# Two-block network on one core: output units of the merge as 512 + 256 columns, an earlier table load with six stores, and half-row transposes in the linear attention

## The reference

```
mixed = (sigmoid(g_a) * (y_a @ w_a) + sigmoid(g_b) * (y_b @ w_b))      # 256 x 2048
y = mixed @ w_out
x = rmsnorm(x + gate * y, final_g)
```

## Time and profile before

| | |
|---|---|
| runs | 2350.02 us median of 3 (2348.01 to 2352.76) |
| profiled execution | 2346.09 us, its span 2344.2 us |
| TensorE busy | 2285.3 us (97%), 23364 matmuls |
| VectorE, ScalarE, GpSimd busy | 1223.2, 1178.7, 1342.1 us |
| granted TensorE clock | 0.995 of full speed in the mean |
| DMA | 360.70 MB, 154 GB/s in the mean |

### The profile page before, as it was taken

One profiled execution on the slowest core, in us unless ns is written; L12 is line 12 of the kernel. 1 busy time (PEld: TensorE's weight loads), 2 busy tenths in 40 slices (PEclk: granted clock), 3 DMA queues, 4 the chain that ended last, 5 costly groups with the idle time before them and its releaser, 6 DMA issues.

```text
span 2344.2 us, 60261 instructions
## 1 busy us (share of the span) xinstructions
PE 2285.3 (97%) x23364; PEld 1944.4 (83%) x23364; DVE 1223.2 (52%) x2449; ACT 1178.7 (50%) x1999; POOL 1342.1 (57%) x566
## 2 busy tenths in 40 slices
PE   6999999999999999999999999999999999999997
PEld 4787787778777888899999888888888888888886
DVE  2478778877883323466565455453444533333322
ACT  3244545454554444444444555555555555555554
POOL 1112123212332344478888878777777877778785
PEclk8999999999999999999999999999999999999999
DMA  9922112211211223267776555555555555555553
GB/s 389 381 87 66 40 60 77 66 41 58 70 65 50 81 99 108 99 222 251 256 252 244 183 166 176 168 173 173 177 172 171 181 169 172 177 177 172 170 181 134
DMA packets 101244, 360.70 MB, mean 154 GB/s; under 512 B 11184, under 2 KB 14768, under 8 KB 101072
## 3 DMA queue, kind: packets, MB, share of 16 engines
q1 hardware_dynamic: 99872, 356.89, 44.4%
q10 hardware_dynamic: 1200, 1.25, 0.2%
HBM read 356.00 MB, written 2.10 MB: 153 GB/s over the span
## 4 chain that ended last, share of the span: by engine, by line
PE 89%; DVE 2%; ACT 2%; issue 1%; DVEq 0%; ACTq 0%
PE ps L223 32%; PE ps L224 16%; PE ps L684 5%; PE ps L196 4%; PE ps L198 4%; PE ps L197 4%; PE ps L686 4%; PE ps L685 4%; PE ps L815 1%; PE ps L800 1%; PE ps L836 1%; PE ps L980 1%; PE ps L850 1%; PE ps L951 1%; PE ps L1000 1%
## 5 line engine op out<-in xcount | busy, mean ns | idle before, releaser
L187 POOL TENSOR_TENSOR wlo<-raw,whi 128x1024 fp32r<-128x1024 f32 x555 | 1336.7, 2422 | 948.7 <-ACT whi L178 898.7
L223 PE MATMUL ps<-acts,whi 128*128 128x512 f32 x3072 | 1087.6, 398 | 1.3 <-DVE acts L2794 1.3
L224 PE MATMUL ps<-acts,wlo 128*128 128x256 f32 x3072 | 856.7, 279 | 0.0
L178 ACT ACTIVATE whi<-raw 128x1024 fp32r<-128x1024 f32 x562 | 591.6, 1054 | 267.1 <-PE ps L224 138.3
L223 PEld LDWEIGHTS ps<-acts,whi 128*128 128x128 f32 x3072 | 576.2, 188 | 131.6 <-DVE acts L2794 1.6
L224 PEld LDWEIGHTS ps<-acts,wlo 128*128 128x128 f32 x3072 | 579.0, 188 | 0.9
L684 PE MATMUL ps<-acts,whi 128*128 128x512 f32 (+1 forms) x560 | 216.9, 387 | 0.9 <-DVE W L1560 0.9
L686 PE MATMUL ps<-acts,wlo 128*128 128x512 f32 (+1 forms) x560 | 190.1, 339 | 0.0
L685 PE MATMUL ps<-acts,whi 128*128 128x512 f32 (+1 forms) x560 | 189.8, 339 | 0.0
L196 PE MATMUL ps<-acts,whi 128*128 128x256 f32 (+1 forms) x576 | 181.7, 315 | 0.0
L198 PE MATMUL ps<-acts,wlo 128*128 128x256 f32 (+1 forms) x576 | 180.0, 313 | 0.0
(11 more groups left out here) (391 smaller groups left out, 3087.8 us busy)
## 6 DMA issues: line engine op xcount, KB each, us to landing
raw<-stream SPq DMA_DIRECT2D x564, 512.0 KB, 3.3
W<-stream SPq DMA_DIRECT2D x64, 512.0 KB, 9.1
graw<-stream SPq DMA_DIRECT2D x32, 512.0 KB, 4.3
W<-xT SPq DMA_DIRECT2D x4, 1024.0 KB, 8.7
XR<-xT SPq DMA_DIRECT2D x16, 128.0 KB, 5.7
outT<-XR SPq DMA_DIRECT2D x4, 512.0 KB, 3.3
cns<-consts SPq DMA_DIRECT2D x1, 928.0 KB, 11.1
cns<-consts SPq DMA_DIRECT2D x1, 896.0 KB, 7.4
```

What stands on the lines that cost most here:

```text
L178: nc.scalar.activation(high, raw[slot], ACT.Copy).then_inc(hi_done, 1)
L187: nc.gpsimd.tensor_tensor(wlo[slot], raw[slot], whi[slot].bitcast(F32), ALU.subtract).then_inc(lo_done, 1)
L223: nc.tensor.matmul(both_parts, whi[slot][:, k, :], hl[:, :, k0 + k, :], start=first and k == 0, stop=False)
L224: ins = nc.tensor.matmul(ps[:, bank, 0:T], wlo[slot][:, k, :], hl[:, 0, k0 + k, :], start=False, stop=last and k == UK - 1)
```

## The change

Three edits, independent of each other. In the merge the two output units use `mm_wide` with the y activations; ScalarE copies the upper halves of their two banks after a wait for the unit's use, and VectorE adds them before it multiplies. In the linear attention each transpose is made as two of 64 rows, which write 64 columns each into two different banks; the ScalarE copies read the pieces back in order. At the end the one-column Ln comes ahead of the last tile's activations; VectorE's first four tiles and GpSimd's four are scaled in twos, and six stores replace four.

```
--- before.py
+++ after.py
@@ -1759,16 +1759,15 @@
                 tile(10, ps[:, 4, T:], 0)
                 G["vf_ok"].wait(pe, 2 * i + 2)
                 G["gl1"].wait(pe, 2 * i + 2)
-                for c in range(4):
-                    for m in range(2):
-                        o = (c % 2) * T + m * P
-                        ins = nc.tensor.transpose(ps[:, 5 + c // 2, o:o + P], VF[:, m * 512 + c * P:m * 512 + c * P + P],
-                                                  ident)
+                for c, m, r in itertools.product(range(4), range(2), range(2)):
+                    o = (c * 2 + m) * C
+                    ins = nc.tensor.transpose(ps[:, 5 + r, o:o + C], VF[side(r), m * 512 + c * P:m * 512 + c * P + P],
+                                              ident[side(r), side(r)])
                 ins.then_inc(G["vt_mm"].sem, 1)
                 G["ks_ok"].wait(pe, i + 1)
-                for d in range(2):
-                    for c in range(4):
-                        ins = nc.tensor.transpose(ps[:, 2 + d, c * P:c * P + P], KS[:, d, c * P:c * P + P], ident)
+                for d, c, r in itertools.product(range(2), range(4), range(2)):
+                    o = (d * 4 + c) * C
+                    ins = nc.tensor.transpose(ps[:, 2 + r, o:o + C], KS[side(r), d, c * P:c * P + P], ident[side(r), side(r)])
                 ins.then_inc(G["kst_mm"].sem, 1)
                 if i + 1 < GH:
                     next_v(0)
@@ -1884,10 +1883,12 @@
                 if i + 1 < GH:
                     hi(15)
                 G["vt_mm"].wait(act, i + 1)
-                nc.scalar.activation(VTG.rearrange("p c f -> p (c f)"), ps[:, 5:7, :].rearrange("p b n -> p (b n)"),
+                nc.scalar.activation(VTG.rearrange("p c (m r f) -> p (c m) r f", r=2, f=C),
+                                     ps[:, 5:7, :].rearrange("p r (x f) -> p x r f", f=C),
                                      ACT.Copy).then_inc(G["vt_ok"].sem, 1)
                 G["kst_mm"].wait(act, i + 1)
-                nc.scalar.activation(KST.rearrange("p d c f -> p (d c f)"), ps[:, 2:4, :].rearrange("p b n -> p (b n)"),
+                nc.scalar.activation(KST.rearrange("p d c (r f) -> p (d c) r f", r=2),
+                                     ps[:, 2:4, :].rearrange("p r (x f) -> p x r f", f=C),
                                      ACT.Copy).then_inc(G["kst_ok"].sem, 1)
                 if i + 1 < GH:
                     hi(16)
@@ -2008,7 +2009,7 @@
                         .then_inc(G["head_done" if m else "const"].sem, 1)
 
 
-        M = counts("m", "yhi ylo x_in c_in tg m1 m2 mix mhi mlo xr gate_in0 gate_in1 gate_acc gate_mm gate_ok gate_lo gate_sum", 1)
+        M = counts("m", "yhi ylo x_in c_in tg m1 m2 mix mhi mlo xr gate_in0 gate_in1 gate_acc gate_mm gate_ok gate_lo gate_sum out_lo out_sum", 1)
         retire(G)
         def act_ysplit(act):
             split_hi(act, (S_MERGE + LEAD) % RING, S_MERGE + LEAD)
@@ -2043,6 +2044,10 @@
         def gate_low(g):
 
             return qk[:, T * g:T * g + T]
+
+        def out_low(u):
+
+            return sqv[:, u, 0:T]
 
         assert M["mix"].base > 1
 
@@ -2061,8 +2066,7 @@
                     M["gate_ok"].wait(pe, i * 2 + n)
                     for u in range(2):
                         M["ylo"].wait(pe, (2, 5)[u])
-                        mm_unit(pe, (b + 4 + u) % RING, i * 12 + (b + 4 + u), ps[:, bank + 2 + u, 0:T], 1, UK * u, True,
-                                True)
+                        mm_wide(pe, (b + 4 + u) % RING, i * 12 + (b + 4 + u), bank + 2 + u, acts[:, :, 1], UK * u, True, True)
                     M["gate_acc"].wait(pe, (i * 2 + n + 1) * KT)
                     nc.tensor.matmul(ps[:, 6 - bank, T:T + 1], gacc, kst_[:, 2:3], start=True, stop=True)\
                         .then_inc(M["gate_mm"].sem, 1)
@@ -2089,6 +2093,10 @@
                     M["gate_sum"].wait(act, i * 4 + 2 * n + 2)
                     nc.scalar.activation(tg[:, n, T:], ps[:, bank + 1, 0:T], ACT.Tanh, scale=0.5).then_inc(M["tg"].sem, 1)
                     hi(k + 5, k + 6)
+                    act.wait_ge(unit_used, i * 12 + (S_MERGE + k + 6))
+                    M["out_sum"].wait(act, i * 4 + 2 * n)
+                    for u in range(2):
+                        parts_copy(act, out_low(u), bank + 2 + u).then_inc(M["out_lo"].sem, 1)
                     M["mix"].wait(act, i * 2 + n + 1)
                     nc.scalar.activation(mhi[:, bass.ds(2 * i + n, 1), :].rearrange("p a t -> p (a t)"), mx[:, n, :],
                                          ACT.Copy).then_inc(M["mhi"].sem, 1)
@@ -2148,6 +2156,9 @@
                     M["tg"].wait(dve, i * 4 + 2 * n + 2)
                     dve.wait_ge(unit_used, i * 12 + (S_MERGE + U_MERGE * n + 6))
                     for g in range(2):
+                        M["out_lo"].wait(dve, i * 4 + 2 * n + g + 1)
+                        parts_sum(dve, out_low(g), 6 - 4 * n + g).then_inc(M["out_sum"].sem, 1)
+                        M["out_sum"].wait(dve, i * 4 + 2 * n + g + 1)
                         nc.vector.scalar_tensor_tensor(tg[:, n, T * g:T * g + T], tg[:, n, T * g:T * g + T], 1.0,
                                                        ps[:, 6 - 4 * n + g, 0:T], ALU.add, ALU.mult)\
                             .then_inc(M["m1"].sem, 1)
@@ -2227,10 +2238,11 @@
                     for k, n in ((3, 0), (4, 1), (5, None), (6, None)):
                         if base != S_OUT3 or i * RING + k < last:
                             hi(i, k)
+                        if i == KT // 2 - 1 and k == (4 if base == S_OUT3 else 5):
+                            nc.scalar.activation(small[:, 106:107], kst_[:, 3:4], ACT.Ln if base == S_OUT3 else ACT.Sqrt)
                         if n is not None:
                             tile(i, n)
                         if i == KT // 2 - 1 and k == 5:
-                            nc.scalar.activation(small[:, 106:107], kst_[:, 3:4], ACT.Ln if base == S_OUT3 else ACT.Sqrt)
                             if base != S_OUT3:
                                 act_root(act, name, width)
                             act_then(act)
@@ -2416,16 +2428,17 @@
             N = S["out3"]
             N["root"].wait(dve, 1)
             N["hhi"].wait(dve, KT)
-            for k in range(4, KT, 4):
-                nc.vector.tensor_tensor(XR[:, k:k + 4, :], XR[:, k:k + 4, :],
-                                        ps[:, 7, 0:T].unsqueeze(1).broadcast_to([P, 4, T]), ALU.mult).then_inc(N["x"].sem, 1)
+            for k, n in ((4, 2), (6, 2), (8, 4), (12, 4)):
+                nc.vector.tensor_tensor(XR[:, k:k + n, :], XR[:, k:k + n, :],
+                                        ps[:, 7, 0:T].unsqueeze(1).broadcast_to([P, n, T]), ALU.mult).then_inc(N["x"].sem, 1)
 
         def pool_final(pool):
             N = S["out3"]
             N["r"].wait(pool, 1)
             N["hhi"].wait(pool, KT)
-            nc.gpsimd.tensor_tensor(XR[:, 0:4, :], XR[:, 0:4, :], sr[:, T:2 * T].unsqueeze(1).broadcast_to([P, 4, T]),
-                                    ALU.mult).then_inc(N["tab"].sem, 1)
+            for k in (0, 2):
+                nc.gpsimd.tensor_tensor(XR[:, k:k + 2, :], XR[:, k:k + 2, :], sr[:, T:2 * T].unsqueeze(1).broadcast_to([P, 2, T]),
+                                        ALU.mult).then_inc(N["tab"].sem, 1)
 
         def rows(v, k):
 
@@ -2815,13 +2828,11 @@
         stored = sem("stored")
 
         def sp_store(sp):
-            for k in (4, 8, 0, 12):
-                if k:
-                    S["out3"]["x"].wait(sp, k // 4)
-                else:
-                    S["out3"]["tab"].wait(sp, 1)
-                sp.dma_start(outT[:, k:k + 4, :], XR[:, k:k + 4, :]).then_inc(stored, 16)
-            sp.wait_ge(stored, 64)
+            for k, n, ready, value in ((4, 2, "x", 1), (6, 2, "x", 2), (0, 2, "tab", 1), (8, 4, "x", 3), (2, 2, "tab", 2),
+                                       (12, 4, "x", 4)):
+                S["out3"][ready].wait(sp, value)
+                sp.dma_start(outT[:, k:k + n, :], XR[:, k:k + n, :]).then_inc(stored, 16)
+            sp.wait_ge(stored, 96)
 
         block = ctx.enter_context(nc.Block())
```

28 lines of the change are left out of this document (14 added, 14 removed).

## The result

The changed kernel is slower: 2355.33 us median (2352.25 to 2358.66, 22 runs) against 2351.35 us (2346.81 to 2356.39, 22 runs) of the kernel before, ratio 1.0018 with a 95% interval of 1.0011 to 1.0024. I had forecast 2344.4 us and a range to 2348.2.

The account below looks back on a forecast made before the run. TensorE's issue was taken to bound the merge, and a serial chain the tail. Terms 3.2 + 0.8 + 1.1 + 0.5 = 5.6 us, subtracted from the 2350.02 us median, gave 2344.4 us, range 2341.8 to 2348.2.

Parts of the forecast that it names:

- Part 1: Merge: output units as 512 + 256 columns instead of three 256-column products save 3.2 us, range 2.9 to 3.6.
- TensorE's waits for a low part in the merge: Merge: the prediction called itself wrong if TensorE waits for a low part anywhere there; no size given.
- 256 x 0.0125 = 3.2 us: Merge: 256 weight tiles each lose one instruction of three, worth 0.0125 us, from distances of 0.3590 and 0.3465 us.
- Rival (c): Merge: a 512-column product into the output banks costs what it saves; gain only 2.4 us, 2347.6 us; chance 0.04.
- The gate loads on SP wait for that accumulation and move by the same amount, inside its slack: Merge: gate loads shift with VectorE's later gate accumulation, which sat idle 4.90 us before each tile's end; costed at nothing.
- Rival (d): Merge: ScalarE waits for the mix before splitting the next tile's first output unit; 8.8 us lost, 2358.8 us; chance 0.04.
- Part 2: Linear attention: half-row transposes save 0.26 us per group, 0.8 us over three groups; bounds -0.6 to 1.4 us.
- My lower bound of -0.6 us: Linear-attention transposes: the result if the changeover is paid at entry and between the two blocks as well.
- Part 3, the table: Tail: Ln's table load moved before the last tile is hidden with 0.3 us to spare; gain 1.1 us, bounds 0.8 to 1.4.
- (b): Tail: Square or Identity isn't in Ln's table, so loads come back; gain 3.4 us, 2346.6 us; chance 0.06.
- (e): Tail: the table switch takes twice its recorded 1.28 us, delaying the last Square; gain 4.8 us, 2345.2 us; chance 0.03.
- The stores: Tail: six stores start the DMA stream 0.55 us sooner and it never runs dry; gain 0.5 us, bounds 0 to 0.6.

Follow-up runs that it names:

- e3: Changed kernel with ScalarE's copies of the output banks put ahead of the split whose raw data comes late; 2348.49 us, ratio 0.9982 to the kernel before.
- e7: Changed kernel with SP loading the weight unit in front of each gate half instead of behind it; 2347.99 us, ratio 0.9989 to the kernel before.
- e2: Changed kernel with the output units' 512 + 256 form undone, transposes and tail edits kept; 2349.93 us, ratio 0.9983 to the kernel before.
- e8: Changed kernel with only the first output unit as 512 + 256 columns, one copy ahead of the late split; 2345.17 us, ratio 0.9977 to the kernel before.

## Why the prediction was wrong

**Part 1** was forecast at -3.2 us and gave +4.85 in the profiles. TensorE's waits for a low part in the merge are a sign of being wrong that the prediction itself names. Two steps failed.

The first is "256 x 0.0125 = 3.2 us" with its range of 2.9 to 3.6. I took 0.3465 us from a stretch where the alternating pair runs at its fast cadence, and took it for the pair's price. It has a second price, 0.3533, which the trace of before also shows, behind the merge (768 counted tiles there), where I did not look. All 48 weight tiles of an output tile at the slow one cost 16 x 0.32 = 5.1 us more: e3 and e7 have 274.99 us where I forecast 269.8. The rewrite turned a merge that was fast by its own sequence into one that is mostly slow, and at the slow price the new form alone loses 1.8 us to the old one, whose 512 + 256 tiles are all fast. Rival (c), that the form costs what it saves, came nearest, at 0.04; it had no mechanism and too small a price.

The second is "The gate loads on SP wait for that accumulation and move by the same amount, inside its slack", and with it "I cost all of this at nothing". I followed the new work forward, to the first output unit of the next tile with its 3.3 us, and missed that it stands behind a split whose raw data comes last. Before, that unit was issued at 1097.30 and split from 1102.19, the tile's end, released by TensorE and not by the load:

```profile
1097.30 0.33 SPq L151 DMA_DIRECT2D raw<-stream  x1
```

```profile
1102.19 1.06 ACT L178 ACTIVATE whi<-raw 128x1024 fp32r<-128x1024 f32 x1 [1.82 <-PE ps L198]
```

With the 4.0 to 5.5 us of such a load in the changed kernel, the slack was under 1 us. The added steps put VectorE's accumulation, and through SP the load, into ScalarE's own queue ahead of the copies. That is a loop, and a loop has no slack to be used up once: its excess returns with each turn. It cost 3.0 us (278.02 - 274.99), and about 4.6 at equal cadence, since a third of the changed kernel's weight tiles were fast; the weight loads' waits of 5.1 us are near that. Rival (d) named the place and the right side, but its price hung on the wrong slack, so I gave it 0.04.

**Part 2** was right in mechanism and too small: 0.43 us per group, not 0.26. Two groups lie 65.20 us apart (878.73 - 813.53, first output product of a projection to the next), before 65.63 (877.88 - 812.25). The 32 halves take 1.14 us, as the second block took 0.50 and not 0.64. By three groups that is 1.3 us, inside my upper bound of 1.4. The changeover behind them is there (the first full product took 0.43 us, before 0.23), and smaller than the gain. My lower bound of -0.6 us doesn't come out of its own terms: with three changeovers of 0.20 us it is 3 x (0.46 - 0.60) = -0.4. The rule of the Trainium skill, that a load of stationary data goes by its columns (TensorE: Matmul & The Clock Gate, Part 2), did not set the pace: 16 half-row transposes, each with a load of 128 columns, took 0.50 to 0.64 us and not the 1.74 of 16 full ones.

**Part 3, the table**: the load was covered, from 2339.55 to 2340.83, and the last Square started at 2341.40, 0.96 us behind the last tile's first addition (2340.44), before 0.97. The Ln starts 2.17 us after the last tile's first addition (2342.61 - 2340.44), before 3.35 (2333.86 - 2330.51): 1.2 us, forecast 1.1. No load came back before Square, Identity or Ln, so rivals (b) and (e) fall, and with (e) the 2.66 us of the Trainium skill for a switch (ScalarE: Activation LUTs, What ACT_TABLE_LOAD costs): 1.28 us and the next activation at once, again.

**The stores**: the DMA was full from about 2346.4 to 2351.7, 5.3 us as before, and its start came 1.6 us after VectorE's, before 2.05. That is 0.4 to 0.5, as forecast. The tail as a whole gave 1.5 us; I had 1.6.

**The sum.** With what the parts gave alone, the merge apart, 2.8 us were to come, and e2 has a ratio of 0.9983, 4.0 us, whose interval reaches down to 1.9. For the changed kernel the merge and the parts give 4.85 - 2.8 = 2.05 us of loss, and the ratio says 4.2 (2.6 to 5.6): 0.5 us or more has no place in the account, and may lie in the cadence behind the merge. The forecast of 5.6 us was in reach with the first part in another form: e8 won 0.0023 of 2351 us, 5.4 us, with an interval of 3.5 to 7.5.

## What to carry to other kernels

Before work is added to an engine in a loop, follow the new wait around until it comes back to itself, through the DMA queue too, and compare the time around with the bound of the loop; slack of one consumer says nothing. An order change on one engine can be the whole difference: the same work ahead of a split that waits for data cost nothing, behind it 3 us. Before a per-instruction price is used in a sum, take its distribution over the whole trace; if it has two values, the sum needs both.

## What the runs showed of the hardware that I had not expected

Alternating 512- and 256-column products, each with its own weights, run at one of two steady distances, 0.3467 or 0.3533 us per pair, at a granted clock of 1.00, with the same operands and no wait. Equal products don't show it: three of 256 columns took 0.358 to 0.360 us in the stretches that I measured, before and after. The grouped form gave 2.79 us per unit, between the two. The choice holds until the sequence breaks, and is partly fixed by the program (the merge before: fast in both executions of it and in e2) and partly not (768 or 1206 slow pairs behind the merge in two executions of one kernel). It is worth 3 us between those two executions, as much as the edits that were to be measured.
